# Modulation without a stage of its own: fp32 column groups, a third in the preceding layer's second norm, the rest in the state-space stage

## What is computed

```
m = silu(c_vec) @ mod_w + mod_b              # mod_w is 1024 x 6144, per layer
sh1, sc1, g1, sh2, sc2, g2 = split(m, 6)     # six vectors of 1024, for c and for c_ctx
h = rmsnorm(x, norm1) * (1 + sc1) + sh1      # needs sh1, sc1 before the mixer
mix = mixer(h)                               # projections, attention, state space, gates
x = x + g1 * mix                             # needs g1 after the state-space branch
h = rmsnorm(x, norm2) * (1 + sc2) + sh2      # needs sh2, sc2
x = x + g2 * expert_choice_ffn(h)            # needs g2 last
```

## Time and profile before

| | us |
|---|---|
| median of 3 runs | 3288.97 (3288.45 to 3289.63) |
| profiled execution, whole | 3288.19 |
| its span, first to last instruction | 3286.4 |
| TensorE busy | 2875.0 (87%) |
| VectorE busy | 2116.4 (64%) |
| ScalarE busy | 1540.3 (47%) |

### The profile page before, as it was taken

The page is one execution under the profiler, slowest core; times in us unless marked ns, Lnnn a source line. Parts: engine busy times, 40 slices in busy tenths (PEclk is TensorE's granted clock), DMA queues, the critical chain, the costliest instruction groups (busy, mean ns, idle before and its releaser), DMA issues. The chain is left out here.

```text
span 3286.4 us, 42511 instructions
## 1 busy us (share of the span) xinstructions
PE 2875.0 (87%) x16356; PEld 2197.9 (67%) x16356; DVE 2116.4 (64%) x2674; ACT 1540.3 (47%) x1722; POOL 418.2 (13%) x150
## 2 busy tenths in 40 slices
PE   6797999888876999999588979997979769999994
PEld 3696778777774666666338967786768546666663
DVE  7323646654835998998473246466457379898983
ACT  5311444432322777777263115444322247777771
POOL 0001000000010233433000010000000103333410
PEclk9898999989986999999798989998989879999997
DMA  9321112221706999999572212121226279999994
GB/s 352 118 78 40 55 52 67 61 63 52 262 1 252 368 385 388 388 389 383 198 292 74 65 48 66 52 65 54 68 97 202 81 260 379 387 386 387 391 367 174
DMA packets 378526, 644.69 MB, mean 196 GB/s; under 512 B 13056, under 2 KB 124672, under 8 KB 377472
## 3 DMA queue, kind: packets, MB, share of 16 engines
q1 hardware_dynamic: 372224, 621.59, 52.3%
q0 software_dynamic: 6144, 20.98, 2.8%
HBM read 591.01 MB, written 51.51 MB: 196 GB/s over the span
## 5 line engine op out<-in xcount | busy, mean ns | idle before, releaser
L2049 DVE TENSOR_TENSOR w_lo<-expert_raw,w_hi 128x2048 fp32r<-128x2048 f32 x384 | 868.0, 2287 | 89.9 <-ACT w_hi L1999 89.6
L1999 ACT ACTIVATE w_hi<-expert_raw 128x2048 fp32r<-128x2048 f32 x384 | 736.6, 1920 | 337.8 <-PE ps L1955 277.7
L1953 PE MATMUL ps<-w_hi,xe_hi 128*80 128x512 f32 x1024 | 407.9, 398 | 11.1 <-DVE xe_lo L2054 11.1
L1954 PE MATMUL ps<-w_lo,xe_hi 128*80 128x512 f32 x1024 | 404.6, 395 | 0.0
L1955 PE MATMUL ps<-w_hi,xe_lo 128*80 128x512 f32 x1024 | 400.4, 391 | 0.0
L1921 POOL DMA_INDIRECT h<-tok_rows,rows x32 | 267.1, 8345 | 289.5 <-DMA sum_rows<-h,rows 181.8
L517 PE MATMUL ps<-h_hi,in_w_hi 128*128 128x320 f32 x640 | 200.1, 313 | 41.1 <-DVE h_lo L569 41.1
L1953 PEld LDWEIGHTS ps<-w_hi,xe_hi 128*80 128x80 f32 x1024 | 152.3, 149 | 92.2 <-DVE xe_lo L2054 11.6
L796 PE MATMUL ps<-h_hi,attention_gate_w_hi 128*128 128x320 f32 x640 | 207.4, 324 | 6.5 <-DVE attention_gate_w_lo L783 6.5
L1955 PEld LDWEIGHTS ps<-w_hi,xe_lo 128*80 128x80 f32 x1024 | 152.5, 149 | 86.2 <-issue 1.6
L1953 PE MATMUL ps<-w_hi,hid_hi 128*80 128x512 f32 x512 | 204.0, 398 | 3.3 <-DVE hid_lo L2073 3.3
(11 more groups left out here) (300 smaller groups left out, 5803.6 us busy)
## 6 DMA issues: line engine op xcount, KB each, us to landing
expert_raw<-in_exp_w_gate SPq DMA_DIRECT2D x64, 2048.0 KB, 10.8
expert_raw<-in_exp_w_up SPq DMA_DIRECT2D x64, 2048.0 KB, 10.1
expert_raw<-in_exp_w_down SPq DMA_DIRECT2D x64, 2048.0 KB, 11.1
mod_raw<-in_mod_w SPq DMA_DIRECT2D x28, 2048.0 KB, 12.1
in_raw<-in_w_mix SPq DMA_DIRECT2D x20, 1024.0 KB, 5.4
attention_gate_raw<-in_w_in SPq DMA_DIRECT2D x80, 256.0 KB, 3.3
gate_tanh_back<-gate_rows SPq DMA_DIRECT2D x64, 320.0 KB, 3.9
gate_rows<-cq SPq DMA_DIRECT2D x40, 320.0 KB, 2.2
```

Source lines behind the costliest of these rows:

```text
L1953: pe.matmul(ps[0:SLOTS, bank, :], hi[:, k, :], whi[:, s, w, :], start=(k == 0), stop=False)
L1954: pe.matmul(ps[0:SLOTS, bank, :], hi[:, k, :], wlo[:, s, w, :], start=False, stop=False)
L1999: act.activation(whi[:, (2 * i + kh) % SPLIT], raw[:, i % RAW, KH * kh:KH * kh + KH], ACT.Copy).then_inc(hi_ready, 1)
L2049: v.tensor_tensor(wlo[:, s], raw[:, i % RAW, KH * kh:KH * kh + KH], whi[:, s].bitcast(F32), ALU.subtract).then_inc(lo_ready, 1)
```

## The change

The stage `modulation` goes. The weights are no longer split: they are multiplied in fp32 as they come, 128 columns at a time, with a stationary operand of 32 columns of which two hold the condition (`silu`, made once in `begin`). Four such matmuls have their sums in the four groups of 32 partitions of one bank. VectorE copies the bank to SBUF, and TensorE picks the rows and turns them into columns. The first 16 of the 48 column blocks (sh1 and sc1) of a layer are made in `begin` for the first layer, and in n2 for the layer that comes after (the second layer's n2 makes the first layer's again, and nobody uses them): four units of 512 columns, 2 MB each. The other 32 blocks are made in `ssm` of the same layer, in 16 units of 256 columns, 1 MB each, two a step in steps 2 to 9, with two buffers, one of which lies in `conv_tanh`. `outputs` now has the four matmuls of L1303 first, and then the four of L1304 in the order of heads 0, 3, 2, 1.

```diff
-            modulation(nc, io, g, layer)
...
-            norm(nc, g, "n2", g["gs2"], g["mod"][:, 24:32, :])
+            norm(nc, g, "n2", g["gs2"], g["mod"][:, 24:32, :], ahead=(io, (layer + 1) % DEPTH))
...
 def begin(nc, io, g):
...
+            sp.dma_start(cond[:], io["cond"]).then_inc(cond_loaded, 16)
+            rest.start(sp, g["cst"][:], io["cst"])
+            for i in range(MOD_A):
+                part.load(sp, i)
+            sp.dma_start(vec[:], layer_row(io["vec"], 0)).then_inc(vec_loaded, 16)
+            rest.start(sp, g["x"][:], io["x"])
+            rest.start(sp, g["fin"][:], io["fin"])
+            sp.wait_ge(rest.sem, rest.total)
...
+            for i in range(MOD_A):
+                part.products(pe, i)
+            pe.wait_ge(rest.sem, 48)
+            for i in range(MOD_A):
+                part.columns(pe, i)
...
+class Modulation:
...
+    def load(self, sp, i):
+        n = len(self.slots)
+        if i >= n:
+            sp.wait_ge(self.sums_done, i - n + 1)
...
+        sp.dma_start(self.slots[i % n], src.rearrange("l (k p) n -> p (l k) n", p=P)[:, :, c:c + self.width]).then_inc(
+            self.raw_loaded[i % n], 16)
+
+    def products(self, pe, i):
+        n, rows = len(self.slots), KD // self.parts
+        pe.wait_ge(self.raw_loaded[i % n], 16 * (i // n + 1))
+        if i >= self.banks:
+            pe.wait_ge(self.rows_done, i - self.banks + 1)
+        for kk in range(rows):
+            for q in range(4):
+                k, b = q // self.blocks * rows + kk, q % self.blocks
+                last = pe.matmul(self.sums(i)[32 * q:32 * q + 32], self.g["silu"][:, k, :],
+                                 self.slots[i % n][:, k, b * P:(b + 1) * P], start=(kk == 0), stop=(kk == rows - 1))
+        last.then_inc(self.sums_done, 1)
+
+    def copy(self, v, i):
+        v.wait_ge(self.sums_done, i + 1)
+        if i >= 2:
+            v.wait_ge(self.cols_done, i - 1)
+        v.tensor_copy(self.rows[:, i % 2, :], self.sums(i)).then_inc(self.rows_done, 1)
+
+    def columns(self, pe, i):
+        pe.wait_ge(self.rows_done, i + 1)
...
+        for part in range(self.parts):
+            last = pe.matmul(out, self.rows[:, i % 2, :], picked[:, part * self.blocks:(part + 1) * self.blocks, :],
+                             start=(part == 0), stop=(part == self.parts - 1))
+        last.then_inc(self.cols_done, 1)
+
+    def add_bias(self, v):
...
+        v.wait_ge(self.cols_done, self.n)
+        v.tensor_tensor(self.g["mod"][:, a:z, :], self.columns_place().rearrange("p (a b) -> p a b", b=2),
...
 def norm(nc, g, name, gain, shift, fetch=None, store=None, keep=None, ahead=None):
...
+            if ahead:
+                for i in range(MOD_A):
+                    part.load(sp, i)
+                sp.dma_start(g["vec"][:], layer_row(io["vec"], next_layer)).then_inc(vec_loaded, 16)
...
+            if ahead:
+                for i in range(MOD_A):
+                    part.products(pe, i)
+                for i in range(MOD_A):
+                    part.columns(pe, i)
...
 def ssm(nc, io, g, layer):
...
+        def part_units(s):
+            return [i for i in (2 * s - 4, 2 * s - 3) if 0 <= i < part.n]
...
             gates.load(sp, 1)
+            part.load(sp, 0)
             for c in range(NG // 2):
                 for m in (2 * c + 2, 2 * c + 3):
                     if m < NG:
                         gates.load(sp, m)
                 gates.store(sp, c)
+                if c == 0:
+                    sp.wait_ge(conv_silu, 1)
+                    part.load(sp, 1)
+                for i in (2 * c - 4, 2 * c - 3):
+                    if 2 <= i < part.n:
+                        part.load(sp, i)
...
                 for hd in range(4):
...
-                    pe.matmul(dst, xtok[:, t, 64 * hd:64 * hd + 64], mm[:, s % 2, hd, :], start=True, stop=False)
-                    pe.matmul(dst, state[gl:gl + 64, t // 4, dr, hd % 2, :], cts[gl:gl + 64, s % 2, hd % 2, :], start=False, stop=True)
+                    pe.matmul(dst(hd), xtok[:, t, 64 * hd:64 * hd + 64], mm[:, s % 2, hd, :], start=True, stop=False)
+                for hd in (0, 3, 2, 1):
+                    gl = 64 * (hd // 2)
+                    pe.matmul(dst(hd), state[gl:gl + 64, t // 4, dr, hd % 2, :], cts[gl:gl + 64, s % 2, hd % 2, :], start=False, stop=True)
...
+            def part_unit(units):
+                for i in units:
+                    if i:
+                        part.columns(pe, i - 1)
+                    part.products(pe, i)
 
             for s in range(NS + 2):
                 if s < NS:
                     decays(s)
                 for j in gate_slots(s)[0:1]:
                     gates.half(pe, j)
+                part_unit(part_units(s)[0:1])
                 if s >= 2:
                     outputs(s - 2)
                 for j in gate_slots(s)[1:2]:
                     gates.half(pe, j)
+                part_unit(part_units(s)[1:2])
+            part.columns(pe, part.n - 1)
...
                 if 1 <= s <= NS:
                     mixing(s - 1)
+                for i in part_units(s)[0:1]:
+                    part.copy(v, i)
                 for j in gate_slots(s)[1:2]:
                     if j + 2 < NG:
                         gates.split_lo(v, j + 2)
                 if s >= 2:
                     update(s - 2)
+                for i in part_units(s)[1:2]:
+                    part.copy(v, i)
+            part.add_bias(v)
...
 def add_experts(nc, io, g, layer):
...
-            for n in range(MOD_RAW[1]):
-                load_mod(sp, io, g, (layer + 1) % DEPTH, n)
```

More of the change, by code:

```diff
@@ L168, in build @@
         g["rows_added"] = whole.enter_context(nc.semaphore("rows_added"))
-        for name, slots in (("mod_raw_loaded", 4), ("in_raw_loaded", 2), ("expert_raw_loaded", 4)):
+        for name, slots in (("in_raw_loaded", 2), ("expert_raw_loaded", 4)):
             g[name] = [whole.enter_context(nc.semaphore(f"{name}{i}")) for i in range(slots)]
-        with nc.sbuf_tensor("mod_raw", MOD_RAW, F32) as place:
-            g["mod_raw"] = place
         def tensor(scope, name, shape, dt=F32, side=None):
@@ L222, in build @@
             add_experts(nc, io, g, layer)
-        with nc.sbuf_tensor("mod_raw_last", MOD_RAW, F32):
-            finish(nc, io, g)
-MOD_RAW = [P, 4, KD, 512]
+        finish(nc, io, g)
 IN_RAW, EXPERT_RAW = [P, 2, KD, 2 * P + 4], [P, 4, KD, 512]
 FEATURE_UNITS = FEATURE_CHUNKS // 2
[L233 to L237, removed]
 def in_unit(i):
@@ L263, in begin @@
 def begin(nc, io, g):
+    cond, silu, vec = g["cond"], g["silu"], g["vec"]
     with stage(nc) as (block, sem, sb):
-        sb("mod_raw_begin", MOD_RAW)
-        start_loads = Load(sem("start_loads"))
+        th = sb("cond_tanh", [P, KD, 2])
+        th2 = sb("cond_tanh_gated", [P, KD, 2])
+        raw = sb("begin_mod_raw", [P, MOD_A, KD, 512])
+        part = Modulation(io, g, 0, "begin", sem, sb, 0, MOD_A, 512, [raw[:, i] for i in range(MOD_A)], 0, MOD_A)
+        cond_loaded, vec_loaded, rest = sem("cond_loaded"), sem("begin_vec_loaded"), Load(sem("start_loads"))
+        tanh_done, chain = sem("cond_tanh_done"), Count(sem("begin_vector_chain"))
@@ L314, in _ @@
[L314 to L319, removed]
+            act.wait_ge(cond_loaded, 16)
+            act.activation(th[:], cond[:], ACT.Tanh, scale=0.5).then_inc(tanh_done, 1)
@@ L321, in _ @@
         @block.tensor
         def _(pe):
[L323 to L343, removed]
@@ L344, in _ @@
-            columns(NCH - 1)
+            pe.wait_ge(chain.sem, 3)
+            for i in range(MOD_A):
[3 more added lines that the diff above has]
+                part.columns(pe, i)
         @block.vector
         def _(v):
+            chain.mark(v.memset(silu[:], 0.0))
             v.wait_ge(tanh_done, 1)
-            silu.link(v, v.scalar_tensor_tensor(out=th2[:], in0=th[:], scalar=1.0, in1=g["cond"][:], op0=ALU.add, op1=ALU.mult))
@@ L350, in _ @@
[L350 to L364, removed]
@@ L365, in _ @@
-            copy_rows(NCH - 1)
-            v.wait_ge(cols_done, NCH)
-            v.wait_ge(vec_loaded, 16)
[L368 to L373, removed]
@@ L379, in norm @@
+MOD_AHEAD, MOD_CHUNKS = 16, 48
+MOD_A = MOD_AHEAD // 4
+def norm(nc, g, name, gain, shift, fetch=None, store=None, keep=None, ahead=None):
     ps, x, h, cst = g["ps"], g["x"], g["h"], g["cst"]
@@ L388, in norm @@
         h_prompt_ready, stored, kept = sem(name + "_h_prompt_ready"), sem(name + "_stored"), sem(name + "_x_kept")
+        if ahead:
+            io, next_layer = ahead
+            vec_loaded = sem(name + "_vec_loaded")
+            raw = sb(name + "_mod_raw", [P, MOD_A, KD, 512])
+            part = Modulation(io, g, next_layer, name, sem, sb, 0, MOD_A, 512, [raw[:, i] for i in range(MOD_A)], 2, MOD_A)
         @block.sync
@@ L448, in _ @@
                     v.tensor_tensor(xn[:, k % 4], x[:, k], rstd[:], ALU.mult).then_inc(xn_ready, 1)
+            if ahead:
+                for i in range(MOD_A):
```

(18 more changed lines are left out.)

37 lines of the change are left out of this document (31 added, 6 removed).

## The result

The changed kernel took 3300.40 us (median of 7 runs, 3298.51 to 3302.27), the kernel before 3288.97: ratio 1.0034, 95% interval 1.0023 to 1.0045. The forecast was 3297, with 3235 to 3330 as its range.

A forecast was written before the change was run, and what follows sets the result against it. TensorE was taken to bound the kernel, modulation excepted (VectorE's remainder in step with its loads). 3288.2 - 51.7 (first n1) - 67.1 (second) + 6 (n2) + 125 (waiting steps) - 3.3 (other steps) = 3297 us, range 3235 to 3330.

The forecast's parts named there:

- The new wait: State-space steps 3 to 9, both layers: gate loads behind SP's buffer wait idle TensorE 4.6 us, 14 times.
- The pace behind it: After each idle stretch in the state-space stage TensorE runs at its lower clock, losing 2.4 us, bounds 0 and 2.4.
- The unit: State-space stage: 16 fp32 matmuls of 32 columns plus columns and tile-shape change, 1.9 us, between 1.68 and 2.57.
- Four at once: State-space unit: four column groups run together, so its products take four rounds, 1.03 us, and the unit 1.68.
- the price of a round: Column groups run side by side: 0.361 us for the first round of matmuls, 0.222 for each further one.
- One at a time: Rival: a unit's products don't run side by side; unit 4.34 us, kernel 3381; chance 0.02.
- The other steps: State-space steps without the wait: step 2 +1.5 us, steps 10 and 11 -3.7; with bias and gain -1.65 per layer.
- n1 of the first layer: Without the modulation stage n1 starts at 35.4 instead of 87.18, saving 51.7 us.
- n2: n2 in both layers: products, columns, bias and gain behind the last chunk make it longer, +3 us each.
- the rival of a longer n2: Rival: n2's products and columns at the lower clock make 8 us instead of 3, +10; chance 0.03.
- The loop's return: Second layer: n1 takes the removed stage's place behind the loop's return, at 1642.41, saving 67.1 us.

The follow-up runs named there:

- gates_first: Changed kernel with the odd unit's load moved behind the next two gate loads on SP's queue: 3191.73 us, 0.9703 of before.
- wait_kept: Changed kernel with SP waiting at the same place, but issuing the two gate blocks ahead of the 1 MB load: 3227.62 us, 0.9814 of before.
- copy_first: Changed kernel with VectorE copying the odd unit ahead of the late remainder and the state update: 3252.20 us, 0.9890 of before.
- filled: Changed kernel with 18 extra fp32 matmuls ahead of the columns in steps 3 to 9: 3264.17 us, 0.9921 of before.
- outputs_alone: Kernel before with only the new order of the eight matmuls in `outputs`: 3254.24 us, 0.9904 of before.

## Why the prediction was right, point by point

**The new wait** was the term that decides, and each link of it stood in the trace: gate rounding at 6.61 (forecast 6.2), end of the copy at 9.51 (9.1), idle stretch 4.81 and 4.89 in the two steps shown (4.6), step 19.4 to 20.3 (20.4). The 14 steps cost 121.5 over those before (20.13 each against 11.46), forecast 125. gates_first removes the wait and with it 109 us; wait_kept and copy_first cut the chain at two more links.

**The pace behind it** held: taken at 2.4 from the earlier trace rows; 4.66 at 0.55 is 2.1 lost in the step of the windows above, the step of 20.17 lost 2.7 (less 9.57 up to its columns and 7.92 for what stands behind them at the full clock), and filled gives 2.6 a step back. How soon the clock falls was not known from the earlier trace rows and still isn't: in wait_kept it fell in some steps only.

**The unit** was taken at 1.9 and measured 1.44 at the full clock (half of what a step of 12.43 has beside 0.81, 3.70, 3.71 and 1.32 for `outputs`; columns 0.43, products 1.01). It is the term with the largest miss, below even the lower of its two ends, 1.68. Four at once was right, 1.03 forecast and 1.01 measured; too much were the 0.22 that I took on top of it and the 0.65 for the columns and the tile shape, whose 0.16 rests on a price of 0.20 that no row of the forecast shows. 0.46 twice in each of 14 steps is 13 us, which later columns (9.65 instead of 9.1 on the mean, 8 us) and the clock (2.6 instead of 2.4, 2 us) made up for in part: that is luck. The reading of the earlier trace rows held for matmuls of 64 columns: the four of L1303's kind took 0.58 in outputs_alone, forecast 0.583. For those of 32 columns the price of a round, 0.222 whatever runs in it, was wrong: a matmul alone costs 0.149, a round of two 0.184 (1.47 / 8) and a round of four 0.252 (1.01 / 4). "One at a time" would have made a unit 2.8, not 4.34. For `outputs` the same reading gave 1.4, measured 1.32 (3.24 less the 1.92 of outputs_alone).

**The other steps.** The -3.7 a layer for steps 10 and 11 held (twice 1.92 in outputs_alone). Step 2 was mis-sized with the unit: it took 11.99, +0.5 against 11.46 instead of +1.5. `merge`, taken as unchanged, lasts 1.0 longer in the first layer of the changed kernel (841.69 to 972.04, 130.35, at the clock of 0.94 that outputs_alone shows).

**n1 of the first layer** came at 39.30, not at 35.4. x was some 3 us later than my 32.6 (its last transfer ended at 35.2), and the columns stood behind a wait for all loads, so they began at 35.81, and n1 came 3.5 behind that, where I had 2.8.

**n2** was sized too small. Its last work ended 3.8 behind POOL's last h (1001.9 against 998.1), but to the first instruction of the next stage n2 lasts 31.33 (972.04 to 1003.37) instead of 26.85 (958.25 to 985.10): 4.5 more, and 4.6 in the second layer, where I had 3 each. Its products ran slow behind the waits for chunks, 3.64 for one unit of 32 matmuls instead of 1.9 (granted clock 0.50 from 996.24 to 999.81), as in the upper bound of the term and in the rival of a longer n2. The next stage's first line before, then the changed kernel:

```profile
985.10 1.28 ACT L1742 ACT_TABLE_LOAD   x1 [1.36 <-PEq L107]
```

```profile
996.24 3.64 PE L338 MATMUL ps<-n_mod_raw,silu 128*32 128x128 f32 x64 [1.41 <-DMA n_mod_raw<-in_mod_w]
...
1001.72 0.17 DVE L368 SCALAR_TENSOR_TENSOR gs<-mod,vec 128x16 f32<-128x16 f32 x1
...
1003.37 1.28 ACT L1796 ACT_TABLE_LOAD   x1 [5.88 <-PEq L107]
```

**The loop's return** was taken from the old stage's first ScalarE instruction, 6.6 behind the end of the additions (1635.83 to 1642.41). In the changed kernel n1 starts 4.7 behind them (1653.22 to 1657.89), so the stage gave back 69.5, not 67.1.

**What stays open.** 3.9 us between n1 and the state-space stage, and behind n2, between the router and the additions, -0.9 in the first layer and +1.5 in the second, in stages where the diff changes nothing of the work; no run here tells what they are. The misses have both signs (+3.8, +3.9, -4.8, -1.8, +3.0, -0.4 in the table's order), so that the sum came nearer, 3.4 us from the median, than its terms: that nearness is luck, the deciding term is not.

## What to carry to other kernels

A large load with a wait for a buffer is put behind the small loads that the next step needs, and not ahead of them: here the order of three lines on one queue was worth 109 us, more than the stage that was removed saved in one layer. When work moves into a stage that is bound by one engine, price the queues that it passes besides the work itself: 32 units cost some 46 us of TensorE's time, and the wait, with the clock behind it, 109. A change of several parts is timed in parts, since one of them, the order of `outputs`, was worth 33 us alone, and the sum hid it.

## What was not expected of the hardware

Small fp32 matmuls with 32 stationary columns cost 0.149 each when neighbours lie in the same column group, 0.092 with two groups in turn and 0.063 with four. And TensorE's clock was not the same after equal idle stretches: in wait_kept, after 1.76 in one step it granted 0.71 for the next 5.87, and in the step behind it, of 14.49 with 1.78 idle (14.49 less 12.71 busy), 1.00 throughout. Of the 14 steps there 6 have the fall, after 1.44 to 1.76 of idle, and 8 have none, after 1.52 to 1.79.
